# Two transformer blocks on one core: the moving operand of the big matmuls read in another order of its 16-byte lines

## The chip, the cores and the metric

One NeuronCore of one Trainium2 chip runs the kernel as a single launch. The metric is the device time of one execution in microseconds (us), as the median of three runs. All arrays are float32 in HBM; the host only lays the weights out in tiles.

## The reference, cut to what matters

The program computes two blocks over 256 tokens of width 2048, one after the other. With x of 256x2048:

```
block 1:  h = rmsnorm(x) ;  z = h @ w_in                      (2048 x 10248)
          conv branch, forgetting attention (8 heads), two gates
          x = x + (gc * (conv @ w_conv_out) + ga * (attn @ w_attn_out)) @ w_mix_out
          x = x + relu(rmsnorm(x) @ w_ff1)^2 @ w_ff2          (width 8192)
          x = rmsnorm(x)
block 2:  mod = silu(c) @ w_ada + b_ada                       (2048 x 12288)
          h = rmsnorm(x) * (1 + scale) + shift ;  proj = h @ w_in_2
          attention (8 heads) and a state-space mixer (16 heads)
          x = x + gate * (concat(attn, ssm) @ w_out_2)
          x = x + gate * conv_ffn(h) @ w_down                 (width 2 x 5632, then 5632)
          out = rmsnorm(x)
```

Nearly all arithmetic is in the products with the weight matrices, and the change touches how these are read and written by TensorE.

## The kernel before, in words

Activations live transposed: 128 channels on the partitions, 256 tokens (`T`) along the free dimension. A matrix product over 2048 channels is a sum over 16 chunks (`NC`) of 128 channels. To get near-float32 accuracy from TensorE's one-pass float32r type, each operand is split in a high part and a low part. Three buffers hold such split operands: `H` (normed input), `U` (hidden values) and `B` (branch results), each 16 chunks of 512 elements, the first 256 the high part (`ob(buf, k, 0)`), the last 256 the low part (`ob(buf, k, 1)`). Weights come by DMA into `w_raw`, four slots of 1024 columns (8 weight tiles of 128x128); ScalarE rounds a slot into `w_hi` (L823) and VectorE subtracts to get `w_lo` (L1345).

TensorE's work is in units (`unit`). A unit makes one 128-channel block of a result: for each of two weight slots it runs 8 matmuls with a `w_hi` tile as stationary operand over a whole chunk (512 columns: high part times high weights in columns 0 to 255 of the bank, low part times high weights in columns 256 to 511), then 8 with a `w_lo` tile over the high part (256 columns, added to columns 256 to 511). ScalarE then copies the second half of the bank (L853) and VectorE adds it to the first (L1351). Other forms (`joined_unit`, `first_pair`, `pair_high_first`, `half_unit`, `narrow`) use the same two kinds of matmul, or three of 256 columns, in another order. All go through `mm_lines`, and its matmul has line L334 as every matmul of the program has. `keep_warm` issues matmuls of 512 columns whose operands, both from `wn`, and result are plain contiguous ranges; their result is not used. The order of the work on each engine is written out by hand with semaphores.

A "line" in the code is 4 float32, 16 bytes (`LINE`). Before, the lines of a chunk are not adjacent: line l of chunk k lies 128 k + 3 l lines from the buffer's start, so that three chunks interleave and a buffer needs room for 18 chunks. The four-byte elements of a line are adjacent.

```
area = nc.alloc_sbuf_tensor_at(name, [P, CHAIN_N], F32R, offset=base + at)
return bass.AP(area[:, :].tensor, LINE, [[CHAIN_N, P], [2 * T, NC], [STEP * LINE, LINES], [1, LINE]])
...
def mm_lines(out, lhsT, rhs, start, stop):
    return mm(lines(out), lhsT, rhs, start, stop)
```

So TensorE reads a 512-column moving operand as 128 lines at steps of 3 lines, and writes the bank in plain order. The weight tiles are contiguous, 32 lines each. Where the buffers lie, as the built program places them, in lines modulo 16 (256 bytes): a chunk's first line is at 9 in `H`, `U` and `B` alike, a weight tile's at 4 in `w_hi` and `w_lo` alike (each chunk and each weight tile is a multiple of 16 lines long).

Of the kernel before, what the change touches and what calls it, by code (L numbers as in the profile page):

```python
# [20 lines left out]
F32 = mybir.dt.float32  # L21
F32R = mybir.dt.float32r
# [3 lines left out]
P = 128  # L26
T = 256
D = 2048
NC = D // P
# [13 lines left out]
PIECE = FIRST_CHUNKS * P  # L43
# [22 lines left out]


LINE = 4
STEP = 3
LINES = 2 * T // LINE  # L70
CHAIN_N = NC * 2 * T + (STEP - 1) * 2 * T


GROUP1 = 2 * FF_BLOCKS
# [20 lines left out]
Z_BLOCKS = 44  # L95
# [8 lines left out]
def build(nc, t):  # L104

    with ExitStack() as ctx:
        base = (nc.sbuf_base + 31) // 32 * 32
        ctx.enter_context(nc.sbuf_tensor("arena", [P, 3 * NC * 2 * T + 1024 + (Z_BLOCKS - 32) * T], F32))

        def sb(name, shape, dt=F32):  # L110
            return ctx.enter_context(nc.sbuf_tensor(name, shape, dt))
# [3 lines left out]
        def sem(name):  # L115
            if name not in sems:
                sems[name] = ctx.enter_context(nc.semaphore(name.replace(".", "_")))
            return sems[name]


        def chunks_by_line(name, at):

            area = nc.alloc_sbuf_tensor_at(name, [P, CHAIN_N], F32R, offset=base + at)
            return bass.AP(area[:, :].tensor, LINE, [[CHAIN_N, P], [2 * T, NC], [STEP * LINE, LINES], [1, LINE]])

        H = chunks_by_line("H", 0)
        U = chunks_by_line("U", NC * 2 * T * 4)
        B = chunks_by_line("B", 2 * NC * 2 * T * 4)
        G = nc.alloc_sbuf_tensor_at("G", [P, NC, 2, T], F32, offset=base + NC * 2 * T * 4 + 4096)


        Z = nc.alloc_sbuf_tensor_at("Z", [P, Z_BLOCKS, T], F32, offset=base + 2 * NC * 2 * T * 4 + 4096)
        X = sb("X", [P, NC, T])
        small = sb("small", [P, 496])
        w_raw = sb("w_raw", [P, 4, PIECE])
        w_hi = sb("w_hi", [P, 4, PIECE], F32R)
        w_lo = sb("w_lo", [P, 4, PIECE], F32R)
        ada_w = sb("ada_w", [P, 2, ADA_K])
        c_rows = [Z[:, 40:44, :].rearrange("p a t -> p (a t)"), Z[:, 32:36, :].rearrange("p a t -> p (a t)")]
        vec = sb("vec", [P, VEC_N])  # L140
        con = sb("con", [P, CONST_N])
        ones = sb("ones", [P, P])
        epsb = sb("epsb", [P, 2])
        R = sb("R", [P, T])
        ss = sb("ss", [P, T])
        scratch = sb("scratch", [P, 3072])
        mod = sb("mod", [P, 96])
        g1 = sb("g1", [P, NC])
# [9 lines left out]
        rel = sb("rel", [REL_BUCKETS + 1, 8])  # L158
        relhot = Z[0:REL_BUCKETS + 1, 36:38, :].rearrange("p a t -> p (a t)")[:, 0:REL_W]
        relrow = Z[0:8, 38:40, :].rearrange("p a t -> p (a t)")[:, 0:REL_W]  # L160

# [32 lines left out]
        def pair_at(area, col, size):  # L194
            return [area[:, col:col + size], area[:, col + size:col + 2 * size]]
# [6 lines left out]

        idle = G[:, :, :, :].rearrange("p a b t -> p (a b t)")
        at2 = Tiles(qs=pair_at(idle, 0, T), vtok=pair_at(idle, 512, T), prob=pair_at(idle, 1024, 384),
# [7 lines left out]

        dec_rows = Z[0:SSM_HEADS, 40:42, :].rearrange("p a t -> p (a t)")[:, 0:384]
        dec_cols = small[:, 64:112].rearrange("p (n h) -> p n h", n=3)
# [9 lines left out]
        def flat(ap):  # L224
            return ap.rearrange("p a t -> p (a t)")

        def zb(i, n=1):
            return flat(Z[:, bass.ds(i, n), :])

# [2 lines left out]

        def lines(ap):
            return ap.rearrange("p (l e) -> p l e", e=LINE)

        def whole(buf, k):
            return buf[:, k, :, :]

        def ob(buf, i, part):

            at = slice(part * LINES // 2, (part + 1) * LINES // 2)
            if isinstance(i, int):
                return buf[:, i, at, :]
            return buf[:, bass.ds(i, 1), at, :].rearrange("p a l e -> p (a l) e")

        def gates(m, par):

            if isinstance(m, int) and m >= 14:
                return zb(36 + 2 * (m - 14) + par)
            return flat(G[:, bass.ds(m, 1), par, :])  # L250

# [38 lines left out]
        def _(sp):  # L290
# [33 lines left out]
            for m, size, maker, done in OUT_PARTS:  # L324

                sp.wait_ge(sem(maker), done)
                sp.dma_start(t["out"][:, m:m + size, :], Z[:, m:m + size, :]).then_inc(sem("out_stored"), 16)
            sp.wait_ge(sem("out_stored"), 16 * len(OUT_PARTS))
# [3 lines left out]
        def _(pe):  # L332
            def mm(out, lhsT, rhs, start, stop):
                return nc.tensor.matmul(out, lhsT, rhs, start=start, stop=stop, skip_group_check=True)  # L334

            def mm_lines(out, lhsT, rhs, start, stop):
                return mm(lines(out), lhsT, rhs, start, stop)

            def keep_warm(n):

# [33 lines left out]
            def pair_of_units(pair, *args, **kwargs):  # L374
                for par in range(2):
                    unit(pair, par, *args, **kwargs)
# [16 lines left out]
            def first_pair(pair, chunks, held, operand, done):  # L393
# [3 lines left out]
                def chunk(par, k):  # L397
                    h, c = (0, k) if k < cut else (1, k - cut)
                    lhs = slice(c * P, (c + 1) * P)
                    for part in ((0, 1) if c % 2 == 0 else (1, 0)):  # L400
                        if part == 0:
                            end = mm_lines(bank[par][:, :], w_hi[:, 2 * par + h, lhs], whole(U, k), k == 0, False)
                        else:
                            end = mm_lines(bank[par][:, T:2 * T], w_lo[:, 2 * par + h, lhs], ob(U, k, 0), False, k == chunks - 1)
                    return end
# [27 lines left out]
            def spread(name):  # L433

                pe.wait_ge(sem("norm.inverse"), NTH[name])
                mm(spread_out, ones[:, :], R[:, :], True, True).then_inc(sem("norm.spread"), 1)

# [80 lines left out]
            def attention(name, tl, k_step, k0, v0, fill, out_sem, out0, ahead):  # L518
# [41 lines left out]
                for h in range(N_HEADS):  # L560
                    fill(h, 0)
                    if h + 1 < N_HEADS:
# [7 lines left out]
                      ahead=lambda: pair_of_units(PAIR0["qk"] + 7, H, NC))  # L570
            pair_of_units(PAIR0["branch"], B, NC, "branch.operand", two_banks=True)
            with pe.Fori(1, 8) as i:
                pair_of_units(PAIR0["branch"] + i, B, NC, two_banks=True)
            first_pair(PAIR0["mix"], NC, 2, "merged", 0)
            with pe.Fori(1, 8) as i:
                pair_of_units(PAIR0["mix"] + i, U, NC)

# [8 lines left out]
            def ff2(g, pairs=8):  # L586
                with pe.Fori(0, pairs) as i:
                    pair_of_units(PAIR0["ff"] + 16 * g + 8 + i, U, NC, "ff.u_ready", 16 * g)

# [4 lines left out]
            ff2(FF_GROUPS - 1, 7)  # L594
            unit(PAIR0["ff"] + 16 * FF_GROUPS - 1, 0, U, NC)
            joined_unit(PAIR0["ff"] + 16 * FF_GROUPS - 1, U, NC)

# [138 lines left out]
            def half_unit(pair, slot, half, first=0, end=FIRST_CHUNKS):  # L736
# [3 lines left out]
                for c in range(first, end):  # L740
# [5 lines left out]
                    if c % 2 == 0:  # L746
                        mm_lines(bank[slot][:, :], w_hi[:, slot, lhs], whole(B, k), start, False)
                        last = mm_lines(bank[slot][:, T:2 * T], w_lo[:, slot, lhs], ob(B, k, 0), False, stop)
                    else:
                        mm_lines(bank[slot][:, T:2 * T], w_lo[:, slot, lhs], ob(B, k, 0), False, False)  # L750
                        last = mm_lines(bank[slot][:, :], w_hi[:, slot, lhs], whole(B, k), False, stop)
                if end == FIRST_CHUNKS:
# [57 lines left out]
            spread("n5")  # L810
            mm(bank[6][:, 0:T], ones[:, :], R[:, :], True, True).then_inc(sem("norm.spread"), 1)

# [516 lines left out]
        def _(dve):  # L1329
# [45 lines left out]

            def inverse(name, out=R[:, :], root=std):
                dve.wait_ge(sem("norm.root"), NTH[name])
                v.reciprocal(out, root).then_inc(sem("norm.inverse"), 1)  # L1378
                dve.wait_ge(sem("norm.inverse"), NTH[name])


            def inverse_by_token(name, part=0):

                dve.wait_ge(sem("norm.root"), NTH[name])
                link(v.reciprocal(token_inverse, token_root))
                TT(R[:, :].rearrange("p (b t) -> p b t", b=2), ident.unsqueeze(1).to_broadcast([P, 2, P]),
                   token_inverse.unsqueeze(2).to_broadcast([P, 2, P]), ALU.mult).then_inc(sem("norm.inverse"), 1)
# [30 lines left out]
            first_low(3)  # L1418
            def plain_normed(name, pair, par, out, chunk=None, total=total, scale=R[:, :]):

# [9 lines left out]
            def raw_unit(pair, par):  # L1430

                add_halves(PAIR0["gate"] + pair, par, flat(G[:, pair:pair + 1, par, :]))
                split_low(PAIR0["gate"] + pair + 1, par, 0)
                split_low(PAIR0["gate"] + pair + 1, par, 1)

            def add_squares(n, size, other):
# [14 lines left out]
            dve.wait_ge(sem("vec_landed"), 16)  # L1451
            plain_normed("gate", PAIR0["gate"] + 2, 0, flat(G[:, 2:3, 0, :]))
            dve.wait_ge(sem("bank_read"), 2 + 2 * PAIR0["gate"] + 4)
            first_gates = G[:, 0:2, :, :].rearrange("p a b t -> p (a b) t")
            TT(first_gates, first_gates, R[:, :].unsqueeze(1).to_broadcast([P, 4, T]), ALU.mult)\
                .then_inc(sem("gate.out"), 4)
            link(TT(R_squared, R[:, :], R[:, :], ALU.mult))
            plain_normed("gate", PAIR0["gate"] + 2, 1, flat(G[:, 2:3, 1, :]))
            dve.wait_ge(sem("gate.out"), 6)
# [799 lines left out]
```

## Time and profile before

| | us |
|---|---|
| three runs, median (lowest to highest) | 2445.82 (2445.46 to 2445.92) |
| span of the profiled execution | 2444.7 |
| TensorE busy | 2423.8 (99% of the span) |
| TensorE weight loads busy (beside the matmuls) | 2149.2 (88%) |
| VectorE busy | 1969.0 (81%) |
| ScalarE busy | 1261.4 (52%) |
| GpSimd busy | 89.1 (4%) |
| DMA | 566.81 MB, mean 232 GB/s |

The profiled execution's own time, apart from its span, is not listed beside the runs; its span is 1.1 us under their median. A matmul's recorded duration (386 ns on the page for 512 columns) runs from its start to its modelled end and overlaps the next one. How fast TensorE works is told by the distance between the starts of successive matmuls, which the timeline gives: it merges equal instructions, with the start of the first, the time to the end of the last and their count.

### The profile page before, as it was taken

The page shows a single profiled execution, that of the slowest core. Times are in us where ns is not written, and L with a number is a line of the kernel's source. Part 1 is how long each engine was busy: PE and PEld are TensorE (multiplying, and loading weights), DVE is VectorE, ACT ScalarE, POOL GpSimd, SP SyncE. Part 2 cuts the span into 40 slices and gives each one's busy share as a digit, 9 for nine tenths or more (in the row PEclk, how much of TensorE's full clock was granted, in tenths as well). Part 3 has the DMA queues.
Part 4 walks back from the last instruction along what each step waited for, and adds up shares of the span by engine and source line. Part 5 has one row for each costly group of instructions (what it writes and reads, how often), then busy time and mean ns, then how long its engine had stood idle before and what let it go on. Part 6 is the DMA issues. An engine that isn't in the chain of part 4 may idle for free.

```text
span 2444.7 us, 47745 instructions
## 1 busy us (share of the span) xinstructions
PE 2423.8 (99%) x14373; PEld 2149.2 (88%) x14373; DVE 1969.0 (81%) x3114; ACT 1261.4 (52%) x2038; POOL 89.1 (4%) x109
## 2 busy tenths in 40 slices
PE   8999999999999999999999999999999999999998
PEld 7888888888888888888888988889888888888887
DVE  7778876689987887887898877776887887887886
ACT  6444445565554454554555555565545445445455
POOL 0000001000000000000000105300000000000000
PEclk9999999999999999999999999999999999999999
DMA  7786885657888888888888555555566656656555
GB/s 275 274 282 211 279 284 192 200 190 268 285 292 293 287 291 292 286 293 291 289 288 281 175 177 194 188 171 190 167 187 200 202 180 198 198 178 212 192 176 169
DMA packets 162812, 566.81 MB, mean 232 GB/s; under 512 B 18883, under 2 KB 19452, under 8 KB 162748
## 3 DMA queue, kind: packets, MB, share of 16 engines
q1 hardware_dynamic: 132572, 458.71, 56.4%
q10 hardware_dynamic: 27792, 101.20, 12.5%
q0 software_dynamic: 2384, 6.09, 1.0%
q8 instruction: 35, 0.57, 0.1%
q14 instruction: 29, 0.24, 0.0%
HBM read 563.51 MB, written 2.42 MB: 231 GB/s over the span
## 4 chain that ended last, share of the span: by engine, by line
PE 77%; DVE 4%; issue 2%; ACT 1%; DVEq 0%; DMA 0%; ACTq 0%; SPq 0%
PE bank L334 77%; DVE w_lo L1345 1%; DVE scratch L1994 0%; DVE scratch L1992 0%; DVE scratch L1351 0%; DVE scratch L1997 0%; ACT w_hi L823 0%; DMA w_raw<-in_w_in 0%; DVE Z L1705 0%; DVE H L1714 0%; DVE scratch L2020 0%; ACT U L1297 0%; DVE scratch L2014 0%; DVE scratch L1378 0%; PE bank L678 0%
## 5 line engine op out<-in xcount | busy, mean ns | idle before, releaser
L1345 DVE TENSOR_TENSOR w_lo<-w_raw,w_hi 128x1024 fp32r<-128x1024 f32 (+2 forms) x898 | 1048.0, 1176 | 117.1 <-ACT w_hi L823 107.5
L334 PE MATMUL bank<-H,w_hi 128*128 128x512 f32 (+1 forms) x4480 | 1100.0, 386 | 9.3 <-ACT w_hi L275 8.1
L334 PEld LDWEIGHTS bank<-H,w_hi 128*128 128x128 f32 x4480 | 799.3, 188 | 136.7 <-issue 11.2
L823 ACT ACTIVATE w_hi<-w_raw 128x1024 fp32r<-128x1024 f32 (+2 forms) x898 | 876.4, 1012 | 24.1 <-PE bank L334 8.4
L334 PEld LDWEIGHTS bank<-H,w_lo 128*128 128x128 f32 x4416 | 591.5, 188 | 40.5
L334 PE MATMUL bank<-H,w_lo 128*128 128x256 f32 x4416 | 602.9, 277 | 0.0
L334 PE MATMUL bank<-U,w_hi 128*128 128x512 f32 (+1 forms) x2011 | 501.7, 384 | 0.5 <-DVE U L2022 0.3
L853 ACT ACTIVATE scratch<-bank 128x256 f32<-128x256 f32 x355 | 135.1, 381 | 669.3 <-PE bank L334 668.7
L334 PEld LDWEIGHTS bank<-U,w_hi 128*128 128x128 f32 x2011 | 351.1, 188 | 50.0 <-DVE U L2022 0.6
L334 PEld LDWEIGHTS bank<-U,w_lo 128*128 128x128 f32 x1984 | 275.3, 188 | 23.7
L334 PE MATMUL bank<-U,w_lo 128*128 128x256 f32 x1984 | 282.1, 277 | 0.0
L1364 DVE SCALAR_TENSOR_TENSOR ada_w<-ada_w,Z 128x1024 f32<-128x1024 f32 x192 | 233.9, 1218 | 1.2 <-DVE g L1687 0.7
L1351 DVE TENSOR_TENSOR scratch<-bank,scratch 128x256 f32<-128x256 f32 x307 | 129.7, 422 | 112.2 <-ACT scratch L853 111.3
L334 PE MATMUL bank<-B,w_hi 128*128 128x512 f32 (+1 forms) x528 | 131.8, 381 | 0.0
L334 PEld LDWEIGHTS bank<-B,w_hi 128*128 128x128 f32 x528 | 91.3, 188 | 12.4 <-issue 0.2
L853 ACT ACTIVATE scratch<-bank,mod 128x256 f32<-128x256 f32 x78 | 36.9, 473 | 124.4 <-PE bank L334 124.4
L1950 DVE SCALAR_TENSOR_TENSOR scratch<-bank,mod,scratch 128x256 f32<-128x256 f32 x78 | 37.6, 482 | 70.5 <-ACT scratch L853 70.2
L1297 ACT ACTIVATE U<-scratch 128x256 f32 (+1 forms) x44 | 18.4, 418 | 119.5 <-DVE scratch L2020 119.5
L334 PEld LDWEIGHTS bank<-B,w_lo 128*128 128x128 f32 x512 | 71.7, 188 | 6.3
L334 PE MATMUL bank<-B,w_lo 128*128 128x256 f32 x512 | 74.0, 277 | 0.0
L1292 ACT ACTIVATE scratch<-scratch 128x256 f32<-128x256 f32 x44 | 18.4, 418 | 90.2 <-DVE scratch L1997 90.2
L1994 DVE SCALAR_TENSOR_TENSOR scratch<-scratch,con 128x255 f32<-128x255 f32 x88 | 42.6, 484 | 12.0 <-DVE scratch L1992 3.3
(246 smaller groups left out, 1113.2 us busy)
## 6 DMA issues: line engine op xcount, KB each, us to landing
w_raw<-in_w_ff SPq DMA_DIRECT2D x256, 512.0 KB, 5.0
ada_w<-in_w_ada ACTq DMA_DIRECT2D x192, 512.0 KB, 4.7
w_raw<-in_w_up SPq DMA_DIRECT2D x176, 512.0 KB, 4.5
w_raw<-in_w_z SPq DMA_DIRECT2D x96, 512.0 KB, 4.8
w_raw<-in_w_in SPq DMA_DIRECT2D x88, 512.0 KB, 4.4
w_raw<-in_w_gate SPq DMA_DIRECT2D x64, 512.0 KB, 4.6
w_raw<-in_w_down SPq DMA_DIRECT2D x64, 384.0 KB, 3.2
w_raw<-in_w_down SPq DMA_DIRECT2D x64, 320.0 KB, 3.4
```

What stands on the lines that cost most here:

```text
L334: return nc.tensor.matmul(out, lhsT, rhs, start=start, stop=stop, skip_group_check=True)
L823: A(w_hi[:, slot, 0:cols], w_raw[:, slot, 0:cols], ACT.Copy).then_inc(sem("w_high"), 1)
L853: A(half[par], src[:, T:2 * T], ACT.Copy, scale=scale).then_inc(sem("halves"), 1)
L1292: A(sig[0], conv[0], ACT.Sigmoid).then_inc(sem("up.sig"), 1)
L1297: A(ob(U, i, 0), lines(wide[0]), ACT.Copy).then_inc(sem("u_high"), 1)
L1345: TT(w_lo[:, slot, 0:cols], w_raw[:, slot, 0:cols], w_hi[:, slot, 0:cols].bitcast(F32), ALU.subtract)\
L1351: TT(out, bank[par + 2 * other][:, 0:T], half[par], ALU.add).then_inc(sem("bank_read"), 1)
L1364: STT(ada_w[:, par, :], ada_w[:, par, :], 1.0, c_rows[row], ALU.mult, ALU.mult, accum_out=ada_sum[:, bass.ds(chunk, 1)]).then_inc(sem("ada ...
L1950: STT(total[par], src[:, 0:T], mod[:, bass.ds(gate + block, 1)], half[par], ALU.mult, ALU.add)\
L1994: STT(conv[par][:, 1:T], u[:, 0:T - 1], V("ffn_w", 88 + m), conv[par][:, 1:T], ALU.mult, ALU.add)\
```

## The change

`H`, `U` and `B` become plain contiguous arrays of 16 chunks of 512 elements. `mm_lines` now gives TensorE both the moving operand and the result in four rounds: round a reads lines a, a + 4, a + 8 and so on to the end of the operand, and writes the same lines of the bank, so each result ends where it did before. A 512-column matmul thus has four rounds of 32 lines, a 256-column one four rounds of 16 lines. `w_hi` and `w_lo` get 7 and 15 lines of padding before them. `R` and `ss` move into the gap of 1024 elements between `H` and `U`.

```
-STEP = 3
 LINES = 2 * T // LINE
-CHAIN_N = NC * 2 * T + (STEP - 1) * 2 * T
+AREA_N = NC * 2 * T
+GAP = 1024
+MOVING_AT, HIGH_AT, LOW_AT = 0, 7, 15
...
-            area = nc.alloc_sbuf_tensor_at(name, [P, CHAIN_N], F32R, offset=base + at)
-            return bass.AP(area[:, :].tensor, LINE, [[CHAIN_N, P], [2 * T, NC], [STEP * LINE, LINES], [1, LINE]])
+            area = nc.alloc_sbuf_tensor_at(name, [P, AREA_N], F32R, offset=base + 4 * at)
+            return area[:, :].rearrange("p (k l e) -> p k l e", k=NC, e=LINE)
...
-        w_hi = sb("w_hi", [P, 4, PIECE], F32R)
-        w_lo = sb("w_lo", [P, 4, PIECE], F32R)
+        w_hi, w_lo = (sb(name, [P, LINE * at + 4 * PIECE], F32R)[:, LINE * at:].rearrange("p (s c) -> p s c", s=4)
+                      for name, at in (("w_hi", HIGH_AT), ("w_lo", LOW_AT)))
...
-        R = sb("R", [P, T])
-        ss = sb("ss", [P, T])
+        R = nc.alloc_sbuf_tensor_at("R", [P, T], F32, offset=base + 4 * AREA_N)
+        ss = nc.alloc_sbuf_tensor_at("ss", [P, T], F32, offset=base + 4 * (AREA_N + T))
...
+        def in_turn_of_lines(ap):
+            return ap.rearrange("p (i a) e -> p a i e", a=4)
...
             def mm_lines(out, lhsT, rhs, start, stop):
-                return mm(lines(out), lhsT, rhs, start, stop)
+                return mm(in_turn_of_lines(lines(out)), lhsT, in_turn_of_lines(rhs), start, stop)
```

In the built program, in lines modulo 16, a chunk now begins at 8 in all three buffers and a weight tile at 11 in `w_hi` and in `w_lo` (11 is 13 lines behind 8).

No instruction is added, removed or moved; the forms of the operands change. On TensorE, at the program's start (the first units of the gate stage), before:

```order
L334 MATMUL bank<-H,w_hi 128x512 x8
L334 MATMUL bank<-H,w_lo 128x256 x8
L334 MATMUL bank<-H,w_hi 128x512 x8
L334 MATMUL bank<-H,w_lo 128x256 x8
L334 MATMUL bank<-H,w_hi 128x512 x8
```

and now (the last number is the line's 4 elements, the one before it the lines of a round, then the rounds):

```order
L341 MATMUL bank<-H,w_hi 128x4x32x4 x8
L341 MATMUL bank<-H,w_lo 128x4x16x4 x8
L341 MATMUL bank<-H,w_hi 128x4x32x4 x8
L341 MATMUL bank<-H,w_lo 128x4x16x4 x8
L341 MATMUL bank<-H,w_hi 128x4x32x4 x8
```

The order and the counts are the same. The engines that fill `H`, `U` and `B` write 256 adjacent elements now (128x256) where they wrote 64 lines of 4 (128x64x4).

## Rows read from the trace of the kernel before

**Rows 1.** The profile page: the span, engines' busy time, and the chain's shares.

```profile
span 2444.7 us, 47745 instructions
PE 2423.8 (99%) x14373; PEld 2149.2 (88%) x14373; DVE 1969.0 (81%) x3114; ACT 1261.4 (52%) x2038; POOL 89.1 (4%) x109
...
PE 77%; DVE 4%; issue 2%; ACT 1%; DVEq 0%; DMA 0%; ACTq 0%; SPq 0%
```

**Rows 2.** Who waited for whom, TensorE alone, the longest: total us, times, longest.

```profile
PE bank L334 <- ACT w_hi L275: 8.1, 1, 8.1
```

**Rows 3.** TensorE's groups by form: count | busy us, mean ns | idle before.

```profile
L334 PE MATMUL bank<-H,w_hi 128*128 128x512 f32 x4352 | 1075.7, 389 | 8.9 <-ACT w_hi L275 8.1 <-DVE scratch L1351 0.6
L334 PE MATMUL bank<-H,w_lo 128*128 128x256 f32 x4416 | 602.9, 277 | 0.0
L334 PE MATMUL bank<-U,w_hi 128*128 128x512 f32 x1957 | 493.1, 387 | 0.5 <-DVE U L2022 0.3
L334 PE MATMUL bank<-U,w_lo 128*128 128x256 f32 x1984 | 282.1, 277 | 0.0
L334 PE MATMUL bank<-B,w_hi 128*128 128x512 f32 x496 | 126.6, 388 | 0.0
L334 PE MATMUL bank<-B,w_lo 128*128 128x256 f32 x512 | 74.0, 277 | 0.0
L334 PE MATMUL bank<-H,w_hi 128*128 128x256 f32 x128 | 24.6, 291 | 0.4 <-ACT H L1279 0.4
L334 PE MATMUL bank<-U,w_hi 128*128 128x256 f32 x54 | 8.6, 277 | 0.0
...
L334 PE MATMUL bank<-B,w_hi 128*128 128x256 f32 x32 | 5.1, 277 | 0.0
```

**Rows 4.** TensorE's timeline, first block's feed-forward: start us, us, instruction, count.

```profile
999.93 1.96 PE L334 MATMUL bank<-H,w_hi 128*128 128x512 f32 x8
1001.73 1.08 PE L334 MATMUL bank<-H,w_lo 128*128 128x256 f32 x8
...
1037.91 1.96 PE L334 MATMUL bank<-H,w_hi 128*128 128x512 f32 x8
```

**Rows 5.** TensorE's timeline, start of the second block, 256-column matmuls one by one.

```profile
1345.08 0.42 PE L334 MATMUL bank<-H,w_lo 128*128 128x256 f32 x1
...
1348.71 0.41 PE L334 MATMUL bank<-H,w_hi 128*128 128x256 f32 x1
...
1349.13 0.28 PE L334 MATMUL bank<-H,w_hi 128*128 128x256 f32 x1
...
1351.99 0.28 PE L334 MATMUL bank<-H,w_lo 128*128 128x256 f32 x1
```

**Rows 6.** Busy time in windows: engines (count), clock granted, DMA share, GB/s.

```profile
1342.40:1349.00 6.60, 6.51 (x24) 5.12 (x25) 5.82 (x15) 4.46 (x11) 5.03 (x6) 0.50 0.28 95
1350.00:1356.00 6.00, 6.00 (x55) 6.00 (x55) 5.87 (x16) 1.48 (x4) 0.00 (x0) 1.00 0.02 4
648.00:1328.00 680.00, 679.87 (x4011) 605.39 (x4012) 578.80 (x851) 341.23 (x531) 0.00 (x0) 1.00 0.85 290
```

**Rows 7.** TensorE's timeline: last three of four `keep_warm` matmuls, and their durations (min/median/max).

```profile
1714.08 0.85 PE L334 MATMUL bank<-wn 128*128 128x512 f32 x3
...
L334 PE MATMUL bank<-wn x4: 388/394/580, 1713.7 to 1714.5; 128*128 128x512 f32 x4
```

**Rows 8.** TensorE's timeline: the 16-column weights of `narrow`, and what follows them.

```profile
100.09 3.80 PE L334 MATMUL bank<-H,wn 128*16 128x512 f32 x16
103.73 1.51 PE L334 MATMUL bank<-H,w_hi 128*128 128x512 f32 x6
```

**Rows 9.** ScalarE's groups: same operation, result strided in lines, then contiguous.

```profile
L1067 ACT ACTIVATE U<-scratch 128x256 f32 x64 | 26.8, 418 | 13.9 <-DVE scratch L1639 7.5
L1068 ACT ACTIVATE scratch<-scratch 128x256 f32<-128x256 f32 x64 | 25.7, 402 | 0.0
```

More of the change, by code:

```diff
@@ L106, in build @@
     with ExitStack() as ctx:
-        base = (nc.sbuf_base + 31) // 32 * 32
-        ctx.enter_context(nc.sbuf_tensor("arena", [P, 3 * NC * 2 * T + 1024 + (Z_BLOCKS - 32) * T], F32))
+        base = (nc.sbuf_base + 31) // 32 * 32 + 4 * LINE * MOVING_AT
+        ctx.enter_context(nc.sbuf_tensor("arena", [P, LINE * MOVING_AT + 3 * AREA_N + GAP + (Z_BLOCKS - 32) * T], F32))
         def sb(name, shape, dt=F32):
@@ L121, in chunks_by_line @@
         def chunks_by_line(name, at):
-            area = nc.alloc_sbuf_tensor_at(name, [P, CHAIN_N], F32R, offset=base + at)
-            return bass.AP(area[:, :].tensor, LINE, [[CHAIN_N, P], [2 * T, NC], [STEP * LINE, LINES], [1, LINE]])
+            area = nc.alloc_sbuf_tensor_at(name, [P, AREA_N], F32R, offset=base + 4 * at)
+            return area[:, :].rearrange("p (k l e) -> p k l e", k=NC, e=LINE)
         H = chunks_by_line("H", 0)
[L127 to L132, printed above, removed]
+        U = chunks_by_line("U", AREA_N + GAP)
+        B = chunks_by_line("B", 2 * AREA_N + GAP)
+        G = nc.alloc_sbuf_tensor_at("G", [P, NC, 2, T], F32, offset=base + 4 * (AREA_N + GAP))
+        Z = nc.alloc_sbuf_tensor_at("Z", [P, Z_BLOCKS, T], F32, offset=base + 4 * (2 * AREA_N + GAP))
         X = sb("X", [P, NC, T])
```

## The prediction

> **What bounds the kernel now.** I read the page first: TensorE is busy 99% of the span and the chain that ended last runs through its matmuls for 77% [rows 1]. Then the waits: TensorE's longest total is 8.1 us, once, at the start [rows 2]. So the other engines, at 81% and 52%, are covered nearly everywhere, and the time is a number of matmuls times the distance between their starts (below: the pitch). The list by form gives the numbers: 4352 + 1957 + 496 = 6805 big matmuls of 512 columns, and 4416 + 1984 + 512 of low weights and 128 + 54 + 32 of high weights, together 7126 of 256 columns [rows 3]. The durations in these rows include the overlap with the next matmul and are not used.
>
> The timeline gives the pitch. From 999.93 to 1037.91 us there are 14 rounds of 8 high and 8 low matmuls: 37.98 / 14 = 2.713 us [rows 4]. The 256-column pitch can be read one by one at the start of the second block: 25 steps from 1349.13 to 1351.99 give 0.1144 us [rows 5]; then the 512-column one is 2.713 / 8 - 0.1144 = 0.2247 us. Sum: 6805 x 0.2247 = 1529 us and 7126 x 0.1144 = 815 us, together 2344 of the 2444.7 us. The remaining 100 us are the start, the attention and state-space matmuls, the norms between stages and the end.
>
> How much of a pitch is more than the columns themselves need? Just before 1349 us the granted clock was 0.50 of full speed [rows 6], that is 1.2 GHz instead of 2.4, and the pitch of the same 256-column matmuls was 17 steps from 1345.08 to 1348.71, 0.2135 us each [rows 5], which is 256 columns at 1.2 GHz with nothing left over. At full clock half of that would do: 0.1068 us. The measured 0.1144 has 7.6 ns more. For 512 columns 0.2135 would do, and 0.2247 has 11.2 ns more. This excess is my only source of a gain: 6805 x 11.2 ns = 76 us and 7126 x 7.6 ns = 54 us, 130 us in all.
>
> Is it a matter of how lines are read? Three things speak for it. (1) It does not come from traffic: the 25 steps stand where DMA was at 0.02 of its share, the 14 rounds where it was at 0.85 [rows 6], and both give about 0.115 us for 256 columns. (2) The `keep_warm` matmuls, 512 columns of adjacent lines, are slower: three starts from 1714.08, the last at 1714.08 + 0.85 - 0.39 = 1714.54, give 0.23 us, 5 ns over 0.2247 [rows 7]. So the order of lines and the place of the two operands already move the pitch. (3) With the same reading order of `H` but weight tiles of 16 columns, the 16 steps from 100.09 to 103.73 give 0.2275 us [rows 8]: less weight to load, and yet 3 ns slower. So what is read at the same time by the weight load, and from which lines, matters. The next weights are loaded while a matmul runs; I take the excess for collisions of these two reads, repeated in every matmul because all chunks and tiles have the same place modulo 16 lines.
>
> **The change part by part.** (a) No instruction comes or goes; TensorE's order is the same. (b) `H`, `U` and `B` are written contiguously. ScalarE's square into `U` took 418 ns with strided lines, the same into `scratch` 402 ns contiguous [rows 9]: at most 16 ns on an engine that TensorE covers, so nothing. If ScalarE and VectorE were the bound, some hundreds of such writes would give a few us at most. (c) `R` and `ss` move: nothing, as the same few instructions use them in the same order. (d) The reading order and the places of the weights change together, and this acts on all 13,931 matmuls. (e) The result is written in the same rounds, in pieces of 16 bytes that lie 64 bytes apart, where it was one contiguous range.
>
> (d) and (e) have no row of their own. Bounds: on the good side the whole excess goes, 130 us. On the bad side the pitch gets worse than contiguous reading, priced among the rivals. Between these, the nearest row is contiguous reading. Its excess over 0.2135 is about 16.5 ns; steps of three lines leave 11.2, a step that removed 32%. A second step of that size would give 0.32 x 130 = 42 us, the full one 130. Four rounds by four lines have a regularity that steps of three lack: a round of 32 lines takes 32 x 4 columns / 2.4 GHz = 53 ns, in which a weight load at half a line per moving line passes 16 lines, all places modulo 16 once. So in each round the two streams meet in the same relation, and one fitting offset serves all rounds if the offset is right. I take half of the excess: 6805 x 5.6 ns = 38 us and 7126 x 3.8 ns = 27 us, together 65 us. The pitches would be 0.219 and 0.1106 us.
>
> The trace puts all of it on the path except where another engine takes over. In the densest stage VectorE was busy 578.8 of 680 us, and DMA at 0.85 [rows 6]. Shortened by 2.8% these become 88% and 0.87: still covered. At the ends of stages VectorE's own chain of small steps doesn't shrink with TensorE's pitch; for that I take 1 us off. That leaves 64 us. The sum is made against the profiled span, 2444.7 us, and gives 2380.7; the median of the runs was 1.1 us above the span, so I predict 2381.8, rounded to 2382 us.
>
> One rule says how much of the excess can go at all. The Trainium skill, "TensorE: Matmul & The Clock Gate", section "Wait — 56ns, not 53.3ns?", gives a fixed cost of about 2.5 ns per matmul at the full clock, for 128 as for 512 columns. By it 8.7 and 5.1 ns of the two excesses could go, 59 + 36 = 95 us, and the best case would be 2351 us; the trace agrees in that at half clock nothing was left over, but its excess is three to four times the page's.
>
> **The rivals.** *Collisions gone entirely or nearly.* If the offset of 13 lines is right for both kinds of matmul, 80 to 130 us go: 2316 to 2366 us. For it: the pitch is so steady over 14 rounds that a fixed pattern is at work, which can be avoided as a whole. Against it: the 16-column loads did not make it smaller. 15%.
>
> *No change.* The excess is not collisions of lines but something fixed to float32r streaming, and the difference to `keep_warm` is one of its own operands. Then 2446 us. Against it are the 5 ns between the two [rows 4, 7]. 7%.
>
> *Slower by collisions on reading.* In a round the moving stream comes back to the same place modulo 16 after 4 lines, where steps of three come back after 16. If the weight stream then stands in a place that the round uses, they meet again and again. The point from which this decides: the loss per matmul exceeds what it is now. Priced by the worst arrangement in the trace, contiguous reading: 5.3 ns more on 512 columns and, in proportion to the excess, 3.6 ns more on 256: 36 + 26 = 62 us, 2508 us. 8%.
>
> *Slower by the result.* The bank is written in 128 pieces instead of one range. If each piece cost one column's time more (0.2135 us / 512 = 0.42 ns), a 512-column matmul would lose 53 ns, a 256-column one 27: 361 + 192 = 553 us, about 3000 us. It decides from 0.04 ns per piece, where it eats half of the excess. No row shows a stepped result at full clock; each piece still holds four adjacent values. 10%.
> The Trainium skill, "PSUM — Partial Sum Buffer", section "Specifications (TRN2)", states this rule: PSUM is accessed in lines of 8 bytes, and any non-contiguous pattern slows matmuls significantly. "Advanced Engine Details and Errata", section "PSUM Cachelines", adds that every two consecutive elements should be contiguous, which the pieces of four fulfil; no run here shows it yet.
>
> **How the numbers follow.** A partial gain like my forecast (5 to 80 us) has 60%, the large one 15%, no change 7%, slower 8 + 10 = 18%. A measurement of this kernel can tell a difference of about 0.2%, 5 us. So faster 0.75, same 0.07, slower 0.18. The range leaves out the two slow cases and the far end of the large gain: 2345 to 2451 us.
>
> **What would show it.** Right: the distance between the starts in rows 4 falls from 2.713 us to about 2.64 us for 8 + 8 matmuls, the same in all stages, with the counts unchanged; the 25 steps fall from 0.1144 to about 0.111 us; at half clock the pitch stays 0.2135; `keep_warm` stays at 0.23, since it doesn't use the new order; VectorE's busy time stays at 1969 us and its share grows. Wrong: an unchanged 2.713 (the excess is no matter of lines); a larger pitch in both kinds in proportion to the columns (the result's pieces); a pitch that falls for one kind and rises for the other (the offset fits one only); or an unchanged pitch sum but new waits of TensorE for `w_lo` or `w_hi`, which would mean that VectorE's 88% was not covered.

## The result: slower by 0.24%, and the profile after

The changed kernel takes 2451.16 us (median of 11 runs, 2450.18 to 2452.85), beside 2445.82 us for the kernel before in 11 runs of the same comparison (2444.75 to 2446.99). The ratio is 1.0024, with a 95% interval of 1.0015 to 1.0033: a small loss, but clear of the noise. I had forecast 2382 us; the time lies on the other side of "before" and just past the end of the range, 2451.

The page of the changed kernel, the lines that answer to [rows 1]:

```profile
span 2449.0 us, 47633 instructions
PE 2428.7 (99%) x14373; PEld 2141.8 (87%) x14373; DVE 1968.7 (80%) x3114; ACT 1261.7 (52%) x2038; POOL 89.6 (4%) x109
...
PE 83%; DVE 1%; ACT 0%; issue 0%; DVEq 0%; POOL 0%; ACTq 0%; POOLq 0%
```

The span is 4.3 us longer and TensorE's busy time 4.9 us. TensorE's longest wait is the same 8.1 us at the start. Its groups by form (count | busy us, mean ns | idle before), as in [rows 3]:

```profile
L341 PE MATMUL bank<-H,w_hi 128*128 128x512 f32 x4352 | 1083.1, 389 | 8.8 <-ACT w_hi L282 8.1 <-DVE scratch L1359 0.5
L341 PE MATMUL bank<-H,w_lo 128*128 128x256 f32 x4416 | 597.9, 276 | 0.0
L341 PE MATMUL bank<-U,w_hi 128*128 128x512 f32 x1957 | 495.0, 387 | 0.0
L341 PE MATMUL bank<-U,w_lo 128*128 128x256 f32 x1984 | 281.3, 276 | 0.0
```

The counts are those of before. The time moved both ways: `H` with `w_hi` has 7.4 us more, `H` with `w_lo` 5.0 us less. The timeline shows it in the pitch (start, us, instruction, count), here for the 14 rounds that answer to [rows 4]:

```profile
1000.54 1.98 PE L341 MATMUL bank<-H,w_hi 128*128 128x512 f32 x8
1002.36 1.07 PE L341 MATMUL bank<-H,w_lo 128*128 128x256 f32 x8
...
1038.71 1.98 PE L341 MATMUL bank<-H,w_hi 128*128 128x512 f32 x8
```

A round is (1038.71 - 1000.54) / 14 = 2.726 us, where it was 2.713. Eight high matmuls take 1.82 us (1.80 before), eight low ones 0.90 to 0.91. Summed over all 750 rounds of 8 and 8 from the starts in the trace, the high ones take 12.5 us more and the low ones 4.9 us less; all else together is 3.3 us shorter. That makes the 4.3 us.

Where in a run of eight the loss sits is seen by cutting the timeline at several places. After, one run of high matmuls as a whole, then its last six, its last two, and the start of the low ones that follow (seven of them lie in the window):

```profile
1005.99 1.98 PE L341 MATMUL bank<-H,w_hi 128*128 128x512 f32 x8
...
1006.44 1.53 PE L341 MATMUL bank<-H,w_hi 128*128 128x512 f32 x6
...
1007.37 0.60 PE L341 MATMUL bank<-H,w_hi 128*128 128x512 f32 x2
...
1007.81 0.95 PE L341 MATMUL bank<-H,w_lo 128*128 128x256 f32 x7
```

The same cuts before:

```profile
1005.36 1.96 PE L334 MATMUL bank<-H,w_hi 128*128 128x512 f32 x8
...
1005.81 1.51 PE L334 MATMUL bank<-H,w_hi 128*128 128x512 f32 x6
...
1006.71 0.61 PE L334 MATMUL bank<-H,w_hi 128*128 128x512 f32 x2
...
1007.16 0.62 PE L334 MATMUL bank<-H,w_lo 128*128 128x256 f32 x4
```

Before, the steps are (1005.81 - 1005.36) / 2 = 0.225, (1006.71 - 1005.81) / 4 = 0.225 and (1007.16 - 1006.71) / 2 = 0.225 us: even. After, the first two are 0.225 each, the middle four (1007.37 - 1006.44) / 4 = 0.2325 and the last two 0.22. So the pitch that I had forecast, 0.219, is nearly reached, but only at a run's end; the middle of the run is slower than any step of the run before. From here come the experiments: why does a fixed layout give an uneven pitch?

### The profile page after: what moved, and what is told of

Its sections match the earlier page's. It is cut to its first block, busy times and chain, and to the rows that moved or that the text cites. A ratio compares the mean times of both kernels' runs of the same rounds, so it can differ in the third digit from the quotient of the medians.

```text
span 2449.0 us, 47633 instructions
## 1 busy us (share of the span) xinstructions
PE 2428.7 (99%) x14373; PEld 2141.8 (87%) x14373; DVE 1968.7 (80%) x3114; ACT 1261.7 (52%) x2038; POOL 89.6 (4%) x109
## 4 chain that ended last, share of the span: by engine, by line
PE 83%; DVE 1%; ACT 0%; issue 0%; DVEq 0%; POOL 0%; ACTq 0%; POOLq 0%
PE bank L341 82%; ACT w_hi L831 0%; DVE scratch L1386 0%; PE bank L686 0%; PE bank L553 0%; DVE w_lo L1353 0%; DVE Z L2059 0%; ACT G L1165 0%; DVE scratch L1865 0%; PE bank L630 0%; DVE G L1837 0%; PE bank L544 0%; ACT L1165 0%; ACT L870 0%; DVEq L109 0%
```

## The experiments

**The order alone, in long series.** A kernel with nothing but matmuls: 50 series of 32, one form each, whose lines of operands and result I chose. It leaves the reference's computation out. "Place" is the line, modulo 16, at which a chunk and a weight tile begin: 9 and 4 in the kernel before, 8 and 11 in the changed one. In outline (each series follows one 128-column matmul that marks its start):

```
for name, m_line, order, w_line, result, n, ... in TESTS:      # order: adjacent, by three, four rounds
    for rep in range(4):
        for c in range(8):
            mm(lines(bank, n, result), weight tile c at w_line, lines(move, chunk c at m_line, n, order), c == 0, c == 7)
```

> Only matmuls on filled buffers, nothing of the two blocks is computed: 50 series of 32 matmuls, one per order of the moving lines, order of the result, place and size of the weight tile. Theory R (collisions of the two reads of TensorE): the pitch changes with the reading order and with the place of the weights (adjacent 230, by three 225, four rounds 220 to 235 ns by position for 512 columns), not with the order of the result; with one and the same tile and chunk all positions of a series are alike; with tiles of 16 columns the excess over 213 ns falls by more than half. Theory W (the result's pieces cost): four rounds read with a plain result gives about 219 ns, and any reading with a result in rounds is 5 ns or more slower than with a plain result.

Its timeline (start, us for all 32, bank named after the order <- operands):

```profile
46.58 7.68 PE L125 MATMUL adjacent<-move,weight 128*128 128x512 f32 x32
54.15 7.58 PE L125 MATMUL by_three<-move,weight 128*128 128x512 f32 x32
...
68.99 7.28 PE L125 MATMUL four_rounds<-move,weight 128*128 128x512 f32 x32
76.18 7.27 PE L125 MATMUL four_rounds<-move,weight 128*128 128x512 f32 x32
...
98.44 7.41 PE L125 MATMUL by_three<-move,weight 128*128 128x512 f32 x32
105.74 7.56 PE L125 MATMUL four_rounds<-move,weight 128*128 128x512 f32 x32
```

The first step of a series is slower (266 to 282 ns in four rounds), so the steady pitch is read from single starts. At the changed kernel's place (rows 1 to 4): adjacent 233 ns, by three 227 to 230, four rounds 220.0, both with the plain result (68.99) and with the result in rounds (76.18). At the old place: by three 224.7 (98.44), four rounds 225 and 235 in turn (105.74). For 256 columns four rounds give 113.3 at the new place, by three 114.2 at the old one. So the forecast pitch is nearly there for 512 columns (220.0 for 219), but not for 256 (113.3 for 110.6). The result's pieces cost nothing here: with them the pitch is the same in four rounds and with adjacent lines, and 3 ns lower by three (226.7 beside 230.0). Eight and eight of such matmuls should take 8 x (220.0 + 113.3) = 2667 ns. The kernel takes 2727. The series did not explain the kernel; it left its sequence of forms as the difference.

One expectation failed, and it was the one on the mechanism. With tiles of 16 columns, of which the weight load reads 4 lines instead of 32, the excess of the 512-column matmuls over 213.5 ns was to fall by more than half. At the changed kernel's place the pitch is about 231 ns adjacent, 223 by three and 226 in four rounds, where full tiles give 233, 227 to 230 and 220: a little less excess, somewhat less, and more. For 256 columns it is 113, 113 and 115 ns beside 118, 117 and 113. So the excess does not simply grow with the amount of weights read beside the matmul, and narrow tiles are not slower as such, as [rows 8] had suggested. That the two reads collide is a reading that these series do not show.

**The result in plain order, everything else as changed.**

```
-return mm(in_turn_of_lines(lines(out)), lhsT, in_turn_of_lines(rhs), start, stop)
+return mm(lines(out), lhsT, in_turn_of_lines(rhs), start, stop)
```

> The changed kernel with the moving lines read in four rounds but the result written in plain order (its columns come out permuted, so later values differ; the work is the same). Theory R (reads collide): no change against the changed kernel, 2451 us, 5 us over the kernel before. Theory W (pieces of the result cost what the reading gains): 10 us or more faster than the changed kernel, below 2441 us.

2450.87 us (2449.94 to 2453.4), ratio to before 1.0025 (1.0015 to 1.0034): the changed kernel's time. The result's order costs nothing.

**The result in rounds, in the kernel before.**

```
-return mm(lines(out), lhsT, rhs, start, stop)
+return mm(lines(out).rearrange("p (i a) e -> p a i e", a=4), lhsT, rhs, start, stop)
```

> The kernel before, lines read by three as before, but the result written in four rounds (columns permuted). Theory R: as the kernel before, 2446 us within 2 us, pitch of 8 + 8 matmuls 2.713 us. Theory W: slower by 10 us or more, 2456 us and up.

2445.58 us, ratio 1.0002 (0.9992 to 1.0012). The same from the other side.

**Adjacent lines read in the changed kernel.**

```
-return mm(in_turn_of_lines(lines(out)), lhsT, in_turn_of_lines(rhs), start, stop)
+return mm(lines(out), lhsT, rhs, start, stop)
```

> The changed kernel's layout and places of the weights, but lines read one after the other and the result plain. Theory R: 512 columns at about 230 ns as in keep_warm, so 2446 + 62 = about 2508 us. Theory W, by which reading order matters little and only the result's pieces cost: at or below 2446 us.

2525.87 us (2525.64 to 2526.24), ratio 1.0331 (1.0314 to 1.0349), 18 us more than the 2508 expected. Its timeline:

```profile
1002.34 2.03 PE L341 MATMUL bank<-U,w_hi 128*128 128x512 f32 x8
1004.21 1.11 PE L341 MATMUL bank<-U,w_lo 128*128 128x256 f32 x8
1005.15 2.03 PE L341 MATMUL bank<-U,w_hi 128*128 128x512 f32 x8
```

A round is 2.81 us. The order of reading is worth 75 us at this place (2525.87 - 2450.87, the same kernel with only the reading changed), so the time is a matter of lines; the theory that the excess is fixed falls.

**Rounds of 8 high and 8 low, all places.** Again only matmuls, now in the kernel's sequence: three rounds of 8 high, 8 low for each of the 16 x 16 places of the two kinds of weights.

```
for name, m_line, order, high_line, low_line, mix in TESTS:
    mm(marks, ...)                                             # 128 columns, marks the start
    for rep in range(3):
        for c in range(8): one(order, high_line, 512, c)       # mix "runs"
        for c in range(8): one(order, low_line, 256, c)
```

> Only matmuls, nothing of the blocks is computed. Series of three rounds of 8 high matmuls (512 columns) and 8 low ones (256), as in the kernel: in four rounds and by three lines, for all 16 x 16 places of the high and the low tiles behind the moving lines, and the places of the kernel before and of the changed one. Theory S (a change of form disturbs, and 8 matmuls are too few to settle): at the changed kernel's places 8 high matmuls take about 1815 ns as in the kernel, unequal by position, though 32 of them in a row took 220 ns each; by three lines all positions stay at 225. Over the places the sum of 8 + 8 in four rounds runs from about 2650 to over 2800 ns, and 13 lines behind for both is not its best. Theory K (something else in the kernel, such as the other engines, makes the 229 ns): here the high matmuls take 220 ns at every position and 8 + 8 come to 2667 ns.

Its timeline for the changed kernel's places, the places of before, and the best places (7 lines on for high, 9 for low):

```profile
37.58 1.98 PE L597 MATMUL four_rounds<-move,weight 128*128 128x512 f32 x8
39.40 1.07 PE L597 MATMUL four_rounds<-move,low 128*128 128x256 f32 x8
40.31 1.98 PE L597 MATMUL four_rounds<-move,weight 128*128 128x512 f32 x8
...
45.86 1.96 PE L597 MATMUL by_three<-move,weight 128*128 128x512 f32 x8
...
48.57 1.74 PE L597 MATMUL by_three<-move,weight 128*128 128x512 f32 x7
...
1090.30 1.93 PE L597 MATMUL four_rounds<-move,weight 128*128 128x512 f32 x8
...
1092.98 1.93 PE L597 MATMUL four_rounds<-move,weight 128*128 128x512 f32 x8
```

One round is 2.73, 2.71 and 2.68 us; read in ns from all starts, 2727, 2713 and 2680. Adjacent lines at the changed kernel's places take 2804. The changed kernel's own rounds take 2727, those before 2713 and those with plain reading 2813, so matmuls alone reproduce two of the three exactly and the third within 10 ns. In this kernel no other engine is at work. Busy time in a window of it (us, PE, weight loads, ACT, POOL; clock granted, DMA share, GB/s):

```profile
100.00:4300.00 4200.00, 4200.00 (x24743) 3724.14 (x24742) 0.00 (x0) 0.00 (x0) 1.00 0.00 1
```

TensorE alone, at the full clock, gives the kernel's pitch; what changes it here is the order of the moving lines, the places of the weights and the sequence. Over all places four rounds range from 2680 to 2780 (median 2724), by three from 2706 to 2786 (median 2746).

The single steps show when the loss arises. At the changed kernel's places the first run after the marking matmul steps by 276, 221, 220, 221, 220, 220, 220, 220 ns: the fast pitch. After 8 low ones, the next run steps by 227, 223, 232, 231, 230, 234, 222, 220. The same eight matmuls, the same lines; only what ran before them differs. This is the unevenness seen in the changed kernel at 1005.99.

**High and low in turn, all places.** The same kernel with `mix` "pairs" (one high, one low, and so on), and further orders.

> Only matmuls, nothing of the blocks is computed. As the series before, but high and low matmuls in turn (one of 512, one of 256 columns), for all places, and adjacent lines, 2, 8 and 16 rounds at 16 places. Theory S: in turn every matmul follows one of the other form, so there is no settled state like that of the long series; the sum of a pair depends on the place over a range of 10 ns or more, and at the changed kernel's places it is above 333 ns (220 + 113). Theory K: 333 ns for a pair at the changed kernel's places. No order of rounds gets below 213 + 107 = 320 ns by either theory.

Its timeline at the best places (high 5 lines on, low 14):

```profile
825.27 0.38 PE L720 MATMUL four_rounds<-move,weight 128*128 128x512 f32 x1
...
826.92 0.38 PE L720 MATMUL four_rounds<-move,weight 128*128 128x512 f32 x1
```

Busy time in a window of it, in the same columns:

```profile
300.00:2300.00 2000.00, 2000.00 (x11833) 1777.83 (x11832) 0.00 (x0) 0.00 (x0) 1.00 0.00 1
```

Nothing but TensorE works there, at the full clock. Five pairs take 1.65 us: 330 ns a pair, 221 and 109, so 2640 for eight, better than any order in runs. No other of the 256 places comes below 2666. At the changed kernel's places the pairs settle in one of two states, 2666 for eight in the kernel above and 2720 here. Orders of 8 and 16 rounds, tried at 16 places, are far worse, 2875 to 3342.

**The best places for runs, in the kernel.**

```
-MOVING_AT, HIGH_AT, LOW_AT = 0, 7, 15
+MOVING_AT, HIGH_AT, LOW_AT = 0, 11, 1
```

> The changed kernel with the high tiles 7 and the low tiles 9 lines on from a chunk's first line, modulo 16, instead of 3 and 3; nothing else. Theory S (what a matmul's two reads do to each other depends on the place and on the state that the matmul before left, 256 columns before 512 above all): the series with these places took 2680 ns for 8 + 8 instead of 2727; 47 ns x 850 rounds = 40 us at most below the changed kernel: 2411 to 2425 us. Theory K (the series miss something of the whole kernel): no more than 5 us from 2451 us.

2431.43 us (2429.74 to 2433.35), ratio 0.9944 (0.9927 to 0.996): a gain of 0.6%, but less than expected (2411 to 2425). Its timeline in two stretches:

```profile
998.98 1.93 PE L341 MATMUL bank<-H,w_hi 128*128 128x512 f32 x8
...
1001.66 1.71 PE L341 MATMUL bank<-H,w_hi 128*128 128x512 f32 x7
...
2281.24 1.96 PE L341 MATMUL bank<-H,w_hi 128*128 128x512 f32 x8
2283.96 1.96 PE L341 MATMUL bank<-H,w_hi 128*128 128x512 f32 x8
```

The round is 2.68 us here and 2.72 there, with the same instructions and operands. Of the 750 rounds of 8 and 8, 231 take 2.72. A state once taken lasts for whole stages: from 639 to 1300 us every round that nothing interrupts takes 2.68, from 1635 us on they take 2.72. The expectation had taken the better state everywhere; that is 231 x 0.04 = 9 us of the miss.

**In turn and at the best places for it, in the kernel.** `unit` issues high and low of a chunk one after the other, and so waits for `w_lo` before the first high matmul; only the first pair of units of the program keeps the old sequence.

```
-MOVING_AT, HIGH_AT, LOW_AT = 0, 7, 15
+MOVING_AT, HIGH_AT, LOW_AT = 0, 9, 8
...
+                    pe.wait_ge(sem("w_split"), CREDIT + 4 * pair + 2 * par + h + 1)
...
-                    pe.wait_ge(sem("w_split"), CREDIT + 4 * pair + 2 * par + h + 1)
-                    for c in range(n):
-                        end = low(c)
+                        end = low(c)
```

> The changed kernel with high and low matmuls in turn within a unit (the first pair of units of the program apart) and the tiles at 5 and 14 lines on from the chunk. Theory S: the series gave 2640 ns for 8 + 8, 73 less than the kernel before: 62 us at most, 2384 to 2400 us, pitches 221 and 109 ns. Theory K: no gain over the kernel before, or a loss by waiting for w_lo earlier: 2446 us and above.

**2398.17 us** (2397.94 to 2399.36), ratio 0.9811 (0.9795 to 0.9827). It beats both kernels. The first line of its page:

```profile
span 2396.4 us, 47698 instructions
```

Its longest wait of TensorE after the 8.1 us at the start (total us, times, longest):

```profile
PE bank L341 <- DVE w_lo L1358: 4.2, 10, 1.0
```

Its timeline:

```profile
999.79 0.38 PE L341 MATMUL bank<-H,w_hi 128*128 128x512 f32 x1
...
1000.12 0.38 PE L341 MATMUL bank<-H,w_hi 128*128 128x512 f32 x1
...
1012.00 0.38 PE L341 MATMUL bank<-H,w_hi 128*128 128x512 f32 x1
```

37 pairs in 12.21 us are 330 ns each, as in the kernel of matmuls alone. The wait for `w_lo` now shows with 4.2 us in all.

**In turn, the changed kernel's places.** The edit of `unit` without that of the places.

> The changed kernel at its own places, high and low matmuls in turn. Theory S: the series had two steady states there, 2666 and 2720 ns for 8 + 8, by how they began; so between 2395 us (all in the first) and 2446 us (all in the second), and 2451 us is ruled out. Theory K: 2451 us or above.

2439.5 us (2437.6 to 2443.16), ratio 0.9978 (0.9969 to 0.9988).

```profile
999.67 0.38 PE L341 MATMUL bank<-H,w_hi 128*128 128x512 f32 x1
...
1001.03 0.38 PE L341 MATMUL bank<-H,w_hi 128*128 128x512 f32 x1
```

Four pairs in 1.36 us, 340 ns each. Over the whole trace about two pairs in three take 340 ns, the others 333: mostly the slower of the two states. The expectation had left open which it would be.

**In turn, the kernel before.** The same edit of `unit` in the kernel before.

> The kernel before, lines by three at its own places, high and low matmuls in turn. Theory S: the series gave 2712 ns in turn and 2713 ns in runs, so no change: 2446 us within 3 us. If taking them in turn were a gain by itself (another cause than the state of the reads), it would be as fast as the others in turn. If the earlier wait for w_lo cost something, it would be slower by it.

2449.14 us (2447.56 to 2449.82), ratio 1.0017 (1.0007 to 1.0027). Taking high and low in turn alone brings nothing there; it is 4.6 us slower than the kernel before in the same comparison (2444.56), of which 2.1 us is a new wait of TensorE for `w_lo`.

**Four rounds at the places of before.** The order of the change without its place: the weight tile begins 5 lines behind the chunk, as before.

```
-MOVING_AT, HIGH_AT, LOW_AT = 0, 7, 15
+MOVING_AT, HIGH_AT, LOW_AT = 0, 15, 15
```

> The changed kernel, with both kinds of weight tiles 5 lines behind the chunk's first line modulo 16 as in the kernel before; only the reading order differs from it. The series gave 2699 ns for 8 + 8 with four rounds at this place, 2713 by three lines, 2727 with four rounds at the changed kernel's place. Theory S: 14 ns x 850 rounds = 12 us at most below the kernel before, 2434 to 2441 us, so the new order alone gains a little and the new place gives it back. If the order itself were the loss: 2450 us or above.

2437.71 us (2437.04 to 2438.73), ratio 0.997 (0.9959 to 0.9982).

```profile
999.95 1.95 PE L341 MATMUL bank<-H,w_hi 128*128 128x512 f32 x8
...
1037.75 1.95 PE L341 MATMUL bank<-H,w_hi 128*128 128x512 f32 x8
```

14 rounds in 37.80 us are 2.700 each, what the kernel of matmuls alone gave for this relation (2699). The 2.700 is the mean of rounds of 2.695 and 2.705 that alternate.

**Steps of three at the new places.** The place of the change without its order, in the kernel before: both weights begin 3 lines after the chunk's place, which is the change's 13 behind.

```
-w_hi = sb("w_hi", [P, 4, PIECE], F32R)
-w_lo = sb("w_lo", [P, 4, PIECE], F32R)
+w_hi, w_lo = (sb(name, [P, LINE * at + 4 * PIECE], F32R)[:, LINE * at:].rearrange("p (s c) -> p s c", s=4)
+              for name, at in (("w_hi", 8), ("w_lo", 0)))
```

> The kernel before, lines by three, with both kinds of weight tiles moved to 3 lines on from the chunk's first line, the changed kernel's place. The series by three lines gave about 2753 ns at this place (chunk at line 8) and 2713 at the old. Theory S: 40 ns x 850 rounds = 34 us above the kernel before, 2465 to 2480 us. If the place mattered only together with four rounds: 2446 us.

2511.96 us (2511.86 to 2513.32), ratio 1.0275 (1.0258 to 1.0292): the right sign, and more than twice the size expected.

```profile
1000.12 2.02 PE L334 MATMUL bank<-U,w_hi 128*128 128x512 f32 x8
...
1002.92 1.32 PE L334 MATMUL bank<-U,w_hi 128*128 128x512 f32 x5
```

A round is 2.80 us, where the kernel of matmuls alone had 2753 for the same relation. There the chunk began at line 8, here at 9, so that the relation of the two places is not all that counts; at the old relation the two starts differ as well (2706 and 2713), but by less.

With the last two, order and place can be told apart:

| | places of before | places of the change |
|---|---|---|
| steps of three | 2445.8 us | 2512.0 us |
| four rounds | 2437.7 us | 2451.2 us |

The kernel before took 2445.8 us in the comparison of the changed kernel and 2445.0 in that of the last two; the differences are taken within each comparison. Four rounds are better at either place, by 7 and by 62 us. The new place is worse for either order, by 67 and by 13 us. The change took 7 us with its order and gave 13 back with its place.

## Why the prediction was wrong, and where it was right

**What bounds the kernel: right.** The time is count times pitch. No new wait of any size appeared, VectorE stayed at 1968.7 us, and a fall of the pitch goes to the end nearly in full: in the in-turn version 8 and 8 matmuls take 2640 ns instead of 2713. Over 750 such rounds that is 55 us, of which 46.4 arrived (2444.56 to 2398.17), and 4.2 more are seen in the wait for `w_lo`.

**Parts (a) to (c): right.** Nothing moved. The contiguous write into `U` did not even save the 16 ns: ScalarE's square takes 418 ns as before [rows 9].

```profile
L1075 ACT ACTIVATE U<-scratch 128x256 f32 x64 | 26.8, 418 | 12.1 <-DVE scratch L1647 6.1
```

**Part (e), the result's pieces: right, and the rival falls.** Two kernels and the series show no price. The rule of the Trainium skill, "PSUM — Partial Sum Buffer", section "Specifications (TRN2)", that any non-contiguous pattern slows matmuls significantly, does not hold here: 220.0 ns with pieces of four values as with one range. The line of "Advanced Engine Details and Errata", section "PSUM Cachelines", that every two consecutive elements should be contiguous, is not contradicted; the strong rule stands in that section too, and fares no better there.

**Part (d), the reading order: this is the step that failed.** "So in each round the two streams meet in the same relation, and one fitting offset serves all rounds if the offset is right. I take half of the excess." For a long series of one form the 512-column half came out: 220.0 ns, forecast 219. The 256-column half did not even there: 113.3 from 114.2 ns, 0.9 of the 3.8 ns that the sum took off. So of the two terms of the sum, 38 us had a basis and 27 us did not. In the kernel a run has only eight matmuls. After the change from 256 to 512 columns the run starts at 227 ns, stays at 230 to 234 for four matmuls and reaches 220 at its end; that the change brings the two streams into another relation is how I read this, not something that a run shows. The sum for 512 columns was a forecast of the last two matmuls of a run, applied to all eight. In place of 38 and 27 us gained, the 750 rounds of 8 and 8 show 12.5 us lost and 4.9 gained. I also took for granted that the offset of 13 lines fits, with nothing to test it by; the runs show that the 5 lines of before fit this sequence better (2.700 against 2.726 us a round).

**The argument from proportion.** "A second step of that size would give 0.32 x 130 = 42 us" took what steps of three gain over plain reading for a property of the order. It hangs on the place: in the series it is 6.3 ns for 512 columns at the old places (231.0 to 224.7), which would be 6805 x 6.3 ns = 43 us in the kernel for these matmuls alone, but at the new places the two kernels lie only 14 us apart in all (2525.87 and 2511.96). Nothing could be carried from one order to another by proportion.

**The rivals.** "Slower by collisions on reading" had the right sign, with 8%, and it named what turned out to matter: where the weights stand while the moving operand is read in rounds. But it blamed the rounds, and these gain at both places; the loss comes with the place. Its price was that of another layout, 62 us, and the real one is 5. "No change" is refuted by the kernels with plain reading (+81 us) and at other places (-7 and -13 us). The excess depends on the order of the moving lines and on the places of the weights, as I argued. That it is collisions stays an argument: the 16-column tiles speak against the simple form of it. None of the layouts tried takes it away for 512 columns: the best steady pitch is 220, 6.5 ns over 213.5. The range did not take in a small loss, since I let all of the reading's uncertainty end in a gain or in a great loss. One slip in the prediction carries no weight: its excesses are 4.5 and 3.0 times the 2.5 ns that it sets beside them, not "three to four times".

**The signs I had named.** `keep_warm` and the start of the second block behave as forecast or nearly so:

```profile
1715.18 1.18 PE L341 MATMUL bank<-wn 128*128 128x512 f32 x4
...
1349.32 0.42 PE L341 MATMUL bank<-H,w_lo 128*128 128x256 f32 x1
...
1350.81 0.41 PE L341 MATMUL bank<-H,w_hi 128*128 128x256 f32 x1
...
1352.09 0.28 PE L341 MATMUL bank<-H,w_hi 128*128 128x256 f32 x1
...
1355.96 0.27 PE L341 MATMUL bank<-H,w_hi 128*128 128x256 f32 x1
```

The 7 steps at half clock are 0.213 us each, as before. The 34 steps at full clock are 0.1138 where the 25 before were 0.1144, not 0.111. After its slower first step `keep_warm` has steps of 0.229 and 0.233, as before. And of the marks of failure it was the third that came: the pitch rose for one kind (512 columns) and fell for the other.

**What stays open.** Whether the two reads collide, and in which structure of the chip, was not shown. Why the same instructions settle in one of two states (2.68 and 2.72 us a round in one kernel), and why the loss at the new places with steps of three is so large, is not explained: the expectations from the table over relations held within 7 us of their ranges for five kernels and missed this one by 32.

## What to carry to other kernels

The pitch of matmuls that read plain and rounded lines with weights loaded beside them can hang on the lines of both operands, on the order, and on the matmuls before. Measure a layout in the sequence of forms in which the kernel issues it, for every place: a long series of one form promised 2667 ns a round here, and the kernel took 2727. When a change alters order and place together, run the two apart: the good half (order, -7 us) was hidden by the bad one (place, +13 us), and the best of it (high and low in turn, places 5 and 14, 2398.17 us) lay in neither.

## What was not expected of the hardware

- The pitch depends on what ran before. The same eight 512-column matmuls step by 220 ns, after the first, when one marking matmul stands before them and by up to 234 ns after eight of 256 columns, with no other engine and no DMA at work.
- There are sequences with two steady states: pairs at the changed kernel's places take 2666 or 2720 ns for eight, and in one kernel rounds of 8 and 8 take 2680 ns in some stages and 2720 in others. What decides between them is not known.
- More rounds are not better: at the 16 places tried, 8 and 16 rounds take 2875 to 3342 ns for eight and eight. Four rounds take 2640 to 2892 over all places.
- Weight tiles of 16 columns don't take the excess away. In long series the 512-column pitch is about 231 (adjacent), 223 (by three) and 226 ns (four rounds) with them, and the 256-column one 113 to 115.
